# Last stage of a PEER encoder layer in three pieces: the dense half of the tokens, three gathered blocks, then the last gathered block behind its last rows; TensorE sums no gathered rows

## The reference

```python
def block(args):                       # per block of 128 tokens
    hx, ex, wx = args                  # inputs, picked experts (128, 128), weights
    u_sel = u_tab[ex]
    act = gelu(einsum('td,tjd->tj', hx, u_sel))
    coef = wx * act
    return einsum('tj,tjd->td', coef, v_tab[ex])
...
h = h + g2 * ffn
fsh, fsc = split(c_act @ final_ada_w + final_ada_b, 2)
return _modulate(_rmsnorm(h, final_norm_g), fsh, fsc)   # _rmsnorm(h)*(1+fsc)+fsh
```

## Time and profile before

| | us |
|---|---|
| three timed runs | 2923.24, 2925.75, 2928.24 (median 2925.75) |
| the profiled execution's own time | 2928.15 |
| its span (first to last instruction) | 2926.1 |
| PE busy | 2779.2 (95%) |
| DVE busy | 2238.6 (77%) |
| POOL busy | 1263.6 (43%) |
| ACT busy | 870.2 (30%) |

### The profile page before, as it was taken

One profiled execution on the slowest core, in us unless ns is written; L12 is line 12 of the kernel. 1 busy time (PEld: TensorE's weight loads), 2 busy tenths in 40 slices (PEclk: granted clock), 3 DMA queues, 4 the chain that ended last, 5 costly groups with the idle time before them and its releaser, 6 DMA issues.

```text
span 2926.1 us, 31227 instructions
## 1 busy us (share of the span) xinstructions
PE 2779.2 (95%) x10124; PEld 1513.1 (52%) x10124; DVE 2238.6 (77%) x4600; ACT 870.2 (30%) x1733; POOL 1263.6 (43%) x1089
## 2 busy tenths in 40 slices
PE   6999889899999989999999999989999999999995
PEld 3677677787654434544454545534444444444442
DVE  5998566336799999999998968776776676677675
ACT  3223465333211014754664757800000000000004
POOL 1001111213354554444444445564666566656661
PEclk9999999999999999999999999999999999999997
DMA  5641101234499999999999999999999999999994
GB/s 204 252 173 40 48 30 47 85 135 123 161 406 388 388 379 338 399 383 369 393 360 365 369 400 414 416 407 390 405 402 405 407 397 405 398 402 401 402 393 180
DMA packets 284595, 911.47 MB, mean 311 GB/s; under 512 B 26001, under 2 KB 73361, under 8 KB 277137
## 3 DMA queue, kind: packets, MB, share of 16 engines
q0 software_dynamic: 147456, 536.94, 47.1%
q1 hardware_dynamic: 99632, 297.56, 27.1%
q10 hardware_dynamic: 37344, 74.98, 6.6%
HBM read 826.01 MB, written 83.36 MB: 311 GB/s over the span
## 4 chain that ended last, share of the span: by engine, by line
PE 23%; DMA 20%; DVE 19%; POOL 9%; issue 4%; DVEq 1%; ACT 1%; SPq 1%; ACTq 0%; PEldq 0%; POOLq 0%
DMA s_slot<-in_v,s_row 17%; PE s_pu L1705 16%; DVE s_slot L2166 10%; POOL s_slot L1657 9%; PE s_pw L1742 2%; DMA s_slot<-in_u,s_row 2%; DVE s_hB L2180 2%; PE s_ps L1752 1%; DMA s_wr<-s_w 1%; PE s_pu L340 1%; PE s_pu L341 1%; PE s_pu L344 1%; DVE pk_key L1364 1%; PE s_ps L1826 1%; DVE pk_key L1355 1%
## 5 line engine op out<-in xcount | busy, mean ns | idle before, releaser
L1705 PE MATMUL s_pu<-s_hn,s_ut 128*128 128x512 f32 x2304 | 1007.2, 593 | 4.3 <-ACT s_gst L1857 3.0
L1657 POOL DMA_INDIRECT s_slot<-in_v,s_row x512 | 638.5, 1247 | 372.6 <-DVE s_hB L2180 257.2
L2180 DVE SCALAR_TENSOR_TENSOR s_hB<-s_slot,s_dot,s_hB 128x1024 f32<-128x1024 f32 x469 | 593.3, 1284 | 254.2 <-DMA s_slot<-in_v,s_row 236.3
L1657 POOL DMA_INDIRECT s_slot<-in_u,s_row x512 | 504.6, 986 | 599.0 <-DVE s_slot L2166 521.1
L1705 PEld LDWEIGHTS s_pu<-s_hn,s_ut 128*128 128x128 f32 x2304 | 433.2, 190 | 530.0 <-issue 527.0
L2166 DVE SCALAR_TENSOR_TENSOR s_slot<-s_slot,s_ps 128x1024 f32<-128x1024 f32 x512 | 608.9, 1219 | 80.9 <-DMA s_slot<-in_u,s_row 60.3
L1809 PE MATMUL s_ps<-s_ct,s_vt 128*128 128x512 f32 x1024 | 460.3, 592 | 0.0
L1809 PEld LDWEIGHTS s_ps<-s_ct,s_vt 128*128 128x128 f32 x1024 | 194.6, 190 | 245.0 <-issue 245.0
L1910 ACT ACTIVATE s_hotw<-s_hot,s_rest 128x128 bf16<-128x128 bf16 x1024 | 308.5, 423 | 28.5 <-ACT s_gst L1857 23.7
L1989 ACT ACTIVATE s_sq<-y 128x512 f32<-128x512 f32 x16 | 8.9, 626 | 921.1 <-DVE y L2253 921.1
L1809 PE MATMUL s_pw<-s_ct,s_vt 128*128 128x512 f32 x512 | 246.0, 603 | 24.8 <-DMA s_vt<-in_v_tiles 15.6
(11 more groups left out here) (326 smaller groups left out, 2861.2 us busy)
## 6 DMA issues: line engine op xcount, KB each, us to landing
s_ut<-in_u_tiles SPq DMA_DIRECT2D x128, 512.0 KB, 7.4
s_vt<-in_v_tiles SPq DMA_DIRECT2D x32, 2048.0 KB, 16.9
s_g<-s_gst ACTq DMA_DIRECT2D x120, 256.0 KB, 7.0
s_w<-s_wb ACTq DMA_DIRECT2D x15, 2048.0 KB, 11.7
s_wr<-s_w SPq DMA_DIRECT2D x16, 1920.0 KB, 27.6
s_gr<-s_g SPq DMA_DIRECT2D x60, 512.0 KB, 26.7
s_ada<-in_ada SPq DMA_DIRECT2D x48, 512.0 KB, 6.2
s2w_raw<-in_w_in SPq DMA_DIRECT2D x26, 512.0 KB, 3.6
```

The costliest lines, as they stand in the source:

```text
L1657: pool.indirect_dma_start(out=slot[s][:, :], out_offset=None, in_=io[kind], in_offset=bass.IndirectOffsetOnAxis(ap=row[b][:, j:j + 1], axi ...
L1705: mm = pe.matmul(pu[:, n % 2, :], ut[n % UR][:, k, :], hn[:, k, :], start=(k == 0), stop=(k == DC - 1))
L2180: dve.scalar_tensor_tensor(y, s, dot[b][:, j:j + 1], y, ALU.mult, ALU.add).then_inc(taken, 1)
```

## The change

1. The side path goes: slots, diagonals, `add_side`, `take_y` and their semaphores. All 1024 rows now go through the ring and DVE (`SPARSE_OPS` from 984 to 1024).
2. `wanted` takes 14 rounds of blocks 0 to 2 first (`V_LEAD = 14`), then all four blocks in turn, and ends with 14 rows of block 3 alone.
3. `sparse_by_v` spreads all but the last 12 rows (`BEHIND = 12`) over the 128 tiles of the v sweep. `sparse_by`, and so the 535 rows of the u sweep, stay. The last 12 rows stand between the residual additions.
4. The last stage has three pieces: the dense half (512 tokens), blocks 0 to 2 (384 tokens), and block 3 (128 tokens). For the first two the multiplication by the inverse root moves from DVE to POOL, without the per-channel factor, which ACT's last instruction now applies as its scale. For the third DVE multiplies, four chunks at once, and reads the turned block from PSUM.

The diff, cut to its core:

```diff
-SIDE = 2
-SIDE_ROWS = 40
+LAST = SPARSE - 1
...
-    first = (SIDE_ROWS, 0, 0, 0)
-    for rounds, blocks, skip in ((V_LEAD, 3, (0, 0, 0)), (P - SIDE_ROWS - V_LEAD, 4, (V_LEAD, V_LEAD, V_LEAD, 0))):
...
-V_LEAD = 6
+    if m < V_LEAD * LAST:
+        i, b = divmod(m, LAST)
+        return "v", b, i
+    m -= V_LEAD * LAST
+    if m < (P - V_LEAD) * SPARSE:
+        i, b = divmod(m, SPARSE)
+        return "v", b, i + (0 if b == LAST else V_LEAD)
+    return "v", LAST, P - V_LEAD + m - (P - V_LEAD) * SPARSE
+V_LEAD = 14
+BEHIND = 12
-SPARSE_OPS = 2 * SPARSE * P - SIDE_ROWS
+SPARSE_OPS = 2 * SPARSE * P
...
-            return min(SPARSE_OPS, UNTIL_V + -(-(n + 1) * (SPARSE_OPS - UNTIL_V) // (KEYS - 2)))
+            return UNTIL_V + -(-(n + 1) * (SPARSE_OPS - BEHIND - UNTIL_V) // KEYS)
```

On POOL:

```diff
-                for j in range(SIDE_ROWS):
-                    if side_tile(j) == n + 1:
-                        fetch_side(j)
             for i in range(asked, SPARSE_OPS):
                 fetch(i)
+            for h, each in ((1, 2), (0, 2)):
+                pool.wait_ge(root[h], 1)
+                for k in range(0, DC, each):
+                    part = parts_of_y[h][:, k:k + each, :]
+                    n = part.shape[2]
+                    pool.tensor_tensor(part, part, spread[h][:, :].unsqueeze(1).broadcast_to([P, each, n]), ALU.mult)\
+                        .then_inc(xn_ready[h], each)
```

On PE, where `AHEAD` is `SPARSE_OPS - V_LEAD`:

```diff
-                for j in range(SIDE_ROWS):
-                    if side_tile(j) == n:
-                        add_side(j)
...
-            pe.wait_ge(taken, SPARSE_OPS)
+            pe.wait_ge(taken, AHEAD)
             pe.wait_ge(h2_ready[1], 4)
             for b in range(2):
                 turn_y(b)
+            pe.wait_ge(y_out, 1)
+            turn_y(2)
...
+            squares(1)
+            squares(0)
+            pe.wait_ge(y_out, 2)
+            pe.wait_ge(taken, SPARSE_OPS)
+            turn_y(LAST)
+            squares(2)
```

On ACT:

```diff
+            def shifted(h):
+                for k in range(DC):
+                    act.wait_ge(xn_ready[h], k + 1)
+                    act.activation(parts_of_y[h][:, k, :], parts_of_y[h][:, k, :], ACT.Identity, scale=m.mods[:, 7, k:k + 1],
+                                   bias=m.mods[:, 6, k:k + 1]).then_inc(done[h], 1)
...
             root_of(0)
+            shifted(1)
+            shifted(0)
+            for k in range(0, DC, 4):
+                act.wait_ge(h2_ready[2], k + 4)
+                act.activation(sq[2][:, k:k + 4, :], parts_of_y[2][:, k:k + 4, :], ACT.Square).then_inc(sq_ready[2], 4)
+            root_of(2)
+            shifted(2)
```

On DVE:

```diff
-            dve.wait_ge(side_done, SIDE_ROWS)
...
             for k in range(DC):
                 dve.wait_ge(made, k + 1)
                 residual(1, k)
+                if k % 2 and asked < SPARSE_OPS:
+                    sparse(asked)
+                    asked += 1
             dve.wait_ge(sparse_in, 16)
-            dve.wait_ge(y_out, SPARSE)
             for k in range(DC):
+                if asked < SPARSE_OPS:
+                    sparse(asked)
+                    asked += 1
+                if k == 3:
+                    dve.wait_ge(y_out, LAST)
+                if k >= 3:
+                    residual(0, k - 3)
...
+                residual(2, k)
+            dve.wait_ge(root[2], 1)
+            for k in range(0, DC, 4):
+                last = parts_of_y[2][:, k:k + 4, :]
+                dve.tensor_tensor(last, last, spread[2][:, :].unsqueeze(1).broadcast_to([P, 4, P]), ALU.mult)\
+                    .then_inc(xn_ready[2], 4)
```

More of the change, by code:

```diff
@@ L1465, in step6 @@
     WG = 8
-    slot = [at(f"s6_slot{s}", [P, D], F32, (R0, R0 + 32 * KB, F0 + 64 * KB)[s // 4] + 4 * KB * (s % 4)) for s in range(RING + SIDE)]
+    slot = [at(f"s6_slot{s}", [P, D], F32, (R0, R0 + 32 * KB, F0 + 64 * KB)[s // 4] + 4 * KB * (s % 4)) for s in range(RING)]
     hB = at("s6_hB", [P, SPARSE, D], F32, R0 + 80 * KB)
@@ L1469, in step6 @@
     eq = at("s6_eq", [P, TOPK, P], BF16, R0 + 48 * KB)
-    diag = [at(f"s6_diag{s}", [P, P], F32, R0 + 52 * KB + 512 * s) for s in range(4)]
     q = [at(f"s5_q{s}", [P, HALF], F32, F0 + (32 + 2 * s) * KB) for s in range(2)]
@@ L1487, in step6 @@
     h1_sparse = at("s6_h1_sparse", [P, DC, HALF], F32, R0 + 16 * KB)
[L1488 to L1489 removed]
+    sq = [at(f"s6_sq{h}", [P, DC, n], F32, o)
+          for h, n, o in ((0, LAST * P, R0 + 104 * KB), (1, HALF, F0 + 32 * KB), (2, P, F0 + 8 * KB))]
+    parts_of_y = [y[:, 0, :, 0:LAST * P], y[:, 1, :, :], y[:, 0, :, LAST * P:HALF]]
+    spread = [at(f"s6_spread{h}", [P, n], F32, F0 + 2 * KB * h) for h, n in enumerate((LAST * P, HALF, P))]
     end = 0
@@ L1523, in step6 @@
         ph, py = m.ps
-        landed = [sem(f"s6_landed{s}") for s in range(RING + SIDE)]
-        taken, side_done = sem("s6_taken"), sem("s6_side_done")
+        landed = [sem(f"s6_landed{s}") for s in range(RING)]
+        taken = sem("s6_taken")
         row_ready, ranked = sem("s6_row_ready"), sem("s6_ranked")
@@ L1547, in step6 @@
         h2_ready, sq_ready, ss_ready, root, xn_ready, done, stored = (
-            [sem(f"s6_{n}{h}") for h in range(2)] for n in ("h2", "sqr", "ss", "root", "xn", "done", "st"))
+            [sem(f"s6_{n}{h}") for h in range(3)] for n in ("h2", "sqr", "ss", "root", "xn", "done", "st"))
         wq = Weights(m, sem, "s5w", raw_weights(m, "s5w", F0 + 40 * KB))
@@ L1744, in place_batch @@
                     mm.then_inc(pw_full[unit % 2], 1)
-            def add_side(j):
-                s = RING + j % SIDE
-                pe.wait_ge(landed[s], 16 * (j // SIDE + 1))
-                pe.wait_ge(diag_ready, j + 1)
-                for h in range(2):
-                    c = slice(h * HALF, (h + 1) * HALF)
-                    mm = pe.matmul(py[:, c], diag[j % 4][:, :], slot[s][:, c], start=(j == 0), stop=(j == SIDE_ROWS - 1))
-                mm.then_inc(side_done, 1)
             def scores(h, s):
@@ L1833, in _ @@
                 turn_y(b)
+            pe.wait_ge(y_out, 1)
+            turn_y(2)
             pe.wait_ge(h2_ready[1], 6)
-            squares(1, range(4))
-            for b in range(2, SPARSE):
-                pe.wait_ge(y_out, b - 1)
-                turn_y(b)
-            squares(1, range(4, DC))
-            pe.wait_ge(h2_ready[1], DC)
-            squares(0, range(DC))
+            squares(1)
[4 more added lines that the diff above has]
+            squares(2)
         @block.scalar
@@ L1974, in _ @@
                     evacuate(a, r)
-                for j in range(SIDE_ROWS):
-                    if side_tile(j) == n + 1:
-                        diagonal(j)
-                if n == side_tile(SIDE_ROWS - 1) + 2:
-                    take_y()
             for b in range(done_rows, SPARSE):
@@ L2010, in _ @@
             root_of(0)
-            for h in (1, 0):
-                for k in range(DC):
-                    act.wait_ge(xn_ready[h], k + 1)
-                    act.activation(y[:, h, k, :], y[:, h, k, :], ACT.Identity, bias=m.mods[:, 6, k:k + 1])\
-                       .then_inc(done[h], 1)
+            shifted(1)
[5 more added lines that the diff above has]
+            shifted(2)
         @block.vector
@@ L2177, in sparse @@
                 else:
-                    if j > (0 if b else SIDE_ROWS):
-                        dve.wait_ge(taken, number["v", b, j - 1] + 1)
+                    dve.wait_ge(taken, number["v", b, j - 1] + 1)
                     dve.scalar_tensor_tensor(y, s, dot[b][:, j:j + 1], y, ALU.mult, ALU.add).then_inc(taken, 1)
```

96 lines of the change are left out of this document (36 added, 60 removed).

## The result

The changed kernel took 2964.88 us (median of four runs, 2962.30 to 2967.24), the kernel before 2924.89 in the same group of runs (2923.24 to 2928.24). The ratio is 1.0121, 95% interval 1.0099 to 1.0143: slower, by 40.0 us in the medians. The profiled execution took 2962.8 us, with a span of 2961.0, 34.9 above the 2926.1 of before. The forecast was +28.8 on the span and a time of 2954.5, with a range of its own from 2938 to 2970.

The account below looks back on a forecast made before the run. TensorE was taken to bound the u sweep with VectorE 3.5% below, DMA the v sweep. Terms -18 + 24.8 + 35.5 - 19.5 + 6 = +28.8 gave a span of 2954.9, time 2954.5; own range 2938 to 2970, 8-in-10 range 2927 to 2976.

Parts of the forecast that it names:

- The u sweep: U sweep: VectorE is the second bound and can only drop its waits, so -18 us, between 0 and -40.
- The first rival: U sweep: TensorE alone paces it, so -72 us in place of -18, time 2900.5; chance 0.10.
- The v sweep: V sweep up to its last product: bound by DMA, 19 more rows at 401 GB/s, +24.8 us, between 0 and +39.
- The second rival: V sweep: it has room for the new rows, so 0 in place of +24.8 us, time 2929.7; chance 0.13.
- The third: V sweep: eight slots limit rows to 2.05 us each, +39 in place of +24.8, time 2973; chance 0.13.
- Last product to last row: Behind the v sweep's last product: more rows and residuals on VectorE's queue, +35.5 us, plus +6 for POOL beside VectorE.
- The hold-up: Last stage: POOL's multiplications of the dense half slow VectorE's rows and residuals, +6 us, between 0 and 9.
- Last row to the end: After the last row: ACT's queue is late, 47.5 us becomes 28, so -19.5, between -12 and -27.
- The sum: Whole kernel: all terms together +28.8 us, a span of 2954.9 and a timed median of 2954.5.

Follow-up runs that it names:

- e5: Kernel before, with TensorE multiplying only 128 of the 512 columns of each half of a side row; u sweep 8.0 us shorter.
- e6: Changed kernel, with VectorE taking only 512 of 1024 elements of each u row; u sweep from 1168.3 to 1110.0 us, ratio to before 0.9872.
- e1: Kernel before with only the side path removed, all 1024 rows on VectorE, old last stage; median 2958.5 us, ratio 1.0047.
- e9: e7 with the side path taken away; median 2948.8 us, ratio to the kernel before 1.0032.
- e7: Kernel before, side path kept, with a reordered three-piece last stage and 11 rows behind the sweep; median 2919.3 us, ratio 0.9964.
- e8: Changed kernel, loading only half of each v tile and multiplying that half twice; v sweep 835.5 us instead of 911.2.
- e4: Changed kernel with ten ring slots instead of eight; median 2955.5 us, ratio to the kernel before 1.0041.
- e3: Changed kernel, with POOL's multiplications waiting for the last row and last gathered residual; median 2955.2 us, ratio to the kernel before 1.0042.
- e10: e7, with VectorE multiplying and shifting the three blocks, their roots kept in PSUM; median 2927.4 us, ratio to the kernel before 0.9962.

## Why the prediction was nearly right, point by point

**The u sweep (-18, measured -19.1 at the start of the v sweep).** The step held. VectorE paced the changed sweep, and its waits for batches were all that could go. The rest of TensorE's 72 us became waits of TensorE. Two edits of opposite kind show it: less work on TensorE alone gave 8 to 13.5 us (e5, whose TensorE then waited 34.4 us for side rows), half the elements of VectorE's u rows 58 (e6). 2.6 of the 19.1 us came ahead of the sweep, where nothing was changed; the sweep itself is 17.3 shorter, and the step to the v sweep 0.7 longer. That the number met the forecast within 1.1 us is in part luck. With the side path the sweep took 1185.6 to 1201.1 us in four executions, without it, with eight slots and whole u rows, 1167.7 to 1172.2 in seven, so the gain lies between 13 and 33 us. The first rival (TensorE alone sets the pace) fell.

**The v sweep (+24.8, measured +25.4).** Right in size and in cause. A row added here costs its bytes, 0.524 MB at 401 GB/s or 1.31 us. It came to 1.34 over 19 rows in the changed kernel, 1.19 over 38 in e1 and 1.20 over 37 in e9 against e7. The second rival (room beside TensorE) fell with the rate, which never rose above 401 GB/s in any kernel with the whole table. e8 took the bytes away and got the time back. The third (eight slots) fell with e4. What the forecast did not have is how the price of the rows shows on TensorE. Of the 45.2 us in e1, 27.5 are waits for table tiles (43.1 against 15.6), and some 12 are matmuls that take longer at a lower granted clock (0.98 against 0.99, 0.439 us each against 0.433, over 2048 of them).

**Last product to last row (+41.5, measured +43.0).** The rows and residuals without the hold-up were put at 61.5, and e3 has 61.0. The hold-up was put at 6, as nearly three of four multiplications falling on rows. All four did, at 2.1 us each (2 x 2.08 and 2 x 2.09), so the term is 8.3. The Trainium skill ("SBUF — State Buffer", section "Who interferes with whom") lets VectorE with two SBUF inputs and GpSimd exclude each other for the whole instruction, and the trace agrees: each of POOL's four cost one instruction of VectorE about one of its own durations (9.30 / 4 = 2.3 in e10). The chance average was the mistake, not the mechanism.

**Last row to the end (28, measured 32.9).** This term was mis-sized, and it is most of what was missed. By its own parts (put down first, measured second): until ACT's first shift 6 and 8.1; the shifts of the dense half and three blocks 9 and 10.5; square and sum of the last block 2.2 and 4.4; root 2.4 and 2.2; from there to the end 7.7 and 7.7. They sum to 27.3, which the prediction gave as 28, and to 32.9. Two of the three misses hold sums on TensorE: eight matmuls of 384 columns took 4.60 us and sixteen of 128 columns 3.78. The windows there, and then the same sixteen matmuls in e10 with their window (same columns as above), show why:

```profile
2929.00:2934.00 5.00, 4.74 (x11) 2.77 (x12) 1.24 (x3) 3.16 (x6) 0.00 (x0) 0.62 0.00 0
2947.00:2951.50 4.50, 3.78 (x16) 3.49 (x16) 0.00 (x0) 2.43 (x4) 0.00 (x0) 0.50 0.25 90
...
2899.16 2.58 PE L1847 MATMUL s_ps<-s_sq,ones 128*128 128x128 f32 x16 [2.19 <-ACT s_sq L2040]
...
2899.00:2902.00 3.00, 2.58 (x16) 2.29 (x16) 3.00 (x7) 3.00 (x6) 3.00 (x3) 0.75 0.25 94
```

The granted clock was 0.62 and 0.50, so partly and then wholly its lower level of 1.2 GHz. Ahead of the first TensorE had been busy for 2.1 of 9 us, and ahead of the second idle for 12.6 us. In e10, after 2.2 us of idle time, the granted clock was 0.75, and the sixteen took 2.58 us instead of 3.78. I had priced these sums as if they hid behind the squares. In e7, with the squares ahead of the shifts, the whole term is 23.9.

**The sum.** 28.8 on the span was forecast, 34.9 measured: 1.1 us better at the start of the v sweep, 0.6, 1.5 and 5.0 worse in the other three. In the medians it is +40.0 in the first group and +33.8 in the third. The forecast took the profiled execution to stand 2.4 above the median. It stood 2.1 below it after, which makes the other 4 us between 2954.5 and 2964.88. Why the timed runs of one kernel wander by this much is open. What the runs show is that the slower executions of the kernel before had the lower mean granted clock: in the second group the fastest took 2926.2 us at 0.980 and the slowest 2955.0 at 0.975. Whether the clock is the cause or follows from TensorE's waits can't be told from it.

**What the change gained and lost, all in all.** It gave TensorE 72 us of relief where VectorE allowed 17 of them (13 to 33 by the other profiles). It paid with 40 rows on VectorE where transfers or VectorE bind. The net of the two was a loss of 35 to 36 us between profiled spans with either last stage (e1, and e9 against e7), and of 14 and 21 us between medians of one group (e1, and e9 against e10). The three pieces broke even within 5 us: from the last product to the end they hide work beside rows, but hold VectorE up by 8.3 and keep the last block behind 16 shifts.

## What to carry to other kernels

Before work is taken from the busiest engine, add up busy time, own gaps and waits of the second one over the same stretch: the gain is about its waits, here 20 of 72 us. Work that is moved pays the price of where it lands, so find out what bounds that stretch (here bytes, 1.31 us for each 512 KB) before counting what it leaves. In a last stage, order each queue by what the end waits for: in e7, with the last block's root ahead of 20 shifts and POOL's multiplications behind the last row, the part behind the last row was 9 us shorter than in the changed kernel.
